# Differential attention's output turned one pass later, and sink attention's outputs in two banks

## The chip, the cores and the metric

The kernel runs on one core of one Trainium2 chip. The metric is the device time of one launch in microseconds; a kernel's time is the median of its runs. TensorE's clock is granted at 1.2 or 2.4 GHz, and the profile shows which; PEclk is its mean as a share of 2.4 GHz.

## The reference, cut to what matters

One inference step of a two-layer encoder over 1024 prompt tokens and 8 x 16 sample tokens, D = 1024. Layer 0 mixes differential attention (4 heads) and sliding-window attention with sinks (8 heads in 4 pairs), layer 1 is a chunk-band attention (16 heads in 8 pairs); each layer ends in a ConvFFN. What the change touches is in layer 0:

```
def diff_core(q, k, v, lam, mask):
    s = einsum('bqhcd,bkhcd->bhcqk', q, k) * ATTN_SCALE        # two score maps a head
    p = softmax(where(mask, s, NEG_INF))
    w = p[:, :, 0] - lam * p[:, :, 1]
    return einsum('bhqk,bkhe->bqhe', w, v)

def sink_core(q, k, v, sinks, mask):
    s = einsum('bqngd,bknd->bngqk', qg, k) * ATTN_SCALE
    p = softmax(concatenate([s, sink]))[..., :-1]              # a sink joins the denominator
    return einsum('bngqk,bknd->bqngd', p, v)

# even_mixer
oa = rmsnorm(oa, g_sub) * (1 - lam_init)                       # over a head's 128 columns
y = concatenate([oa, ob], axis=-1) @ w_out
```

All is float32; a matmul of two float32 operands is made of three, with high and low parts (`mm3`, `pair3`).

## The kernel before, in words

The program runs in blocks one after another: set-up with the adaLN projections, attention "AB" (layer 0), ConvFFN, attention "C" (layer 1), ConvFFN, final norm. Within a block each engine has its own instruction stream and waits on semaphores.

Attention handles one head (A, T = 0 to 3) or head pair (B, T = 4 to 7; C, T = 8 to 15) after another. I call them heads 0 to 7. For each, `tile_steps` writes out one list of steps, and every engine walks the same list and emits its part of each step in that order: the order of the list is each engine's order. The list goes in passes u = 0 to 8 over the eight 128-row blocks of queries, and then over the two groups of samples with cached keys (blocks 8 and 9). In pass u stand:

- FA(u-1): VectorE's softmax factors for the block before (L2089 to L2096 for A)
- S(u): scores (TensorE L1699 to L1708), drained by VectorE (L2036, or L2059 for B) and exponentiated by ScalarE (L1886)
- V(u-2): the value product into PSUM bank 7 (`mm3`, L86 to L88, for A; `pair3`, L116 to L118, for B). For A, ScalarE then evacuates it to `osb` (L1900) and squares `osb` (L1917, elementwise result to `osb2`, row sum to `ss`), and VectorE makes the mean (L1986)
- N(u-2), A alone: GpSimd raises the mean to the power -1/2 (L1475), and ScalarE scales `osb` by it into `osb2` (L1854)
- filler: matmuls of the next head's q, k and v projection (L86 to L88 with h and attAB_high), spread over the list
- T(u-1): transposes of the probabilities (L1611), cast by ScalarE to W (L1831), low part Wl by VectorE (L1970)
- O(u-2): for A, TensorE turns `osb2` (L1656, the turn) into columns 256 to 383 of bank 7, ScalarE scales it into `actr` (L1866), VectorE makes the low part `actl` (L1995). For B there is no turn; ScalarE copies out of bank 7 (L1870), VectorE makes the low part (L2000)

A value product waits until the output of the block before has left the bank (`o_bank_free`: `act_low` at least `un(T, u) - 1`). In the stream part, K steps transpose cached keys, and on GpSimd the same K steps issue the loads of cached values (L1372).

R steps are VectorE's rotations (L2020 to L2024) of the next head's q and k. At the end of each of the first seven heads SyncE stores its `actr` and `actl` to memory (L1315, L1316); when head 6 has been stored, six heads are read back into `h` and `hl` (L1325, L1326), and the output projection in head 7 waits for them.

Of the kernel before, what the change touches and what calls it, by code (L numbers as in the profile page):

```python
# [14 lines left out]
P = 128  # L15
# [991 lines left out]
def tile_steps(kind, T, fill, last, nxt):  # L1007
# [5 lines left out]
    late = 0 if fill == "q" else 1  # L1013
    for u in range(QB + 1):
# [7 lines left out]
        body += first + second + ([("V", u - 2)] if u > 1 else [])  # L1022
# [3 lines left out]
        body += ([("N", u - 2)] if u > 1 else []) + one + turned[0:2]  # L1026
        body += ([("O", u - 2)] if u > 1 else []) + two + turned[2:]
    body += [("LB",), ("V", QB - 1)]
    for g in range(2):
        u, x = QB + g, late if g else 1  # L1030
        body += [("K", g, 0), ("K", g, 1), 3 * x, ("N", u - 1), ("SK", g, 0), ("K", g, 2), ("O", u - 1), 2 * x,
# [63 lines left out]
def attention(nc, S, G, ins, outs, kinds):  # L1095
    ctx = ExitStack()
    with ctx:
# [47 lines left out]
        pair_o = ps[:, 7, 0:2 * P]  # L1145
# [101 lines left out]
        def probs_at(kind, T, u, p):  # L1247

            if u >= QB:
                n = 320 if kind == "A" else stream_width(kind)  # L1250
                return slice(0, n), t_banks[:, 0:n]
            n = min(512, (1 if kind == "A" else 2) * width(kind, u) - 512 * p)
            return slice(512 * p, 512 * p + n), ps[:, 5 + t_no(kind, T, u, p) % 2, 0:n]

# [78 lines left out]
        def _(pool):  # L1333
# [92 lines left out]
            def do(what, kind, T, s, c, turns):  # L1426
# [42 lines left out]
                elif what == "N" and kind == "A":  # L1469
# [34 lines left out]
        def _(pe):  # L1504
            spread_pe(pe, S, G, m, F["v"], rs, rs_s)

            def do(what, kind, T, s, c, turns):
# [66 lines left out]
                elif what == "SK":  # L1574
# [4 lines left out]
                    if b == 0:  # L1579
                        pe.wait_ge(S.qz, 2 * T + g + 1)  # L1580
                        pe.wait_ge(S.exps, s_no(T, QB + g - 1, 1 - g))
                    mm = mm3(pe, ps[:, 3, 0:nk], Qz[:, b, :], Qzl[:, b, :], kc[b % 2][:, 0:nk], kcl[b % 2][:, 0:nk],
# [30 lines left out]
                elif what == "V" and s[1] < QB:  # L1613
# [8 lines left out]
                    for j in range(nb):  # L1622
# [3 lines left out]
                        else:  # L1626
                            both, low = (t[:, 0:2 * nb * P].rearrange("p (z x) -> p z x", z=2)[:, :, x] for t in (W, Wl))
                            mm = pair3(pe, pair_o.rearrange("p (z x) -> p z x", z=2), v[:, y], vl[:, y], both, low,
# [23 lines left out]
                elif what == "O" and kind == "A":  # L1652
                    u = s[1]
                    rows = P if u < QB else 64
                    pe.wait_ge(S.o_rows, un(T, u))
                    pe.transpose(ps[:, 7, 256:256 + rows], osb2[0:rows, :], ident[0:rows, 0:rows]).then_inc(S.o_turned, 1)  # L1656
# [13 lines left out]
            def o_bank_free(kind, T, u):  # L1670

                pe.wait_ge(S.act_low, un(T, u) - 1)
# [77 lines left out]
        def _(act):  # L1750
# [12 lines left out]
            def do(what, kind, T, s, c, turns):  # L1763
# [91 lines left out]
                elif what == "O" and (s[1] < QB or kind == "A"):  # L1855
# [11 lines left out]
                    else:  # L1867
                        for z in range(2):
                            r = slice(HD * z, HD * z + HD)
                            i_ = act.copy(act_of(T)[0][r, lo:lo + P], pair_o[r, z * P:(z + 1) * P])  # L1870
# [22 lines left out]
            def outputs(kind, T, u):  # L1893
# [3 lines left out]
                act.wait_ge(S.probs, un(T, u))  # L1897
                if u < QB:
# [17 lines left out]
                if kind == "A":  # L1916
                    act.activation(osb2[0:rows, :], osb[0:rows, :], ACT.Square,  # L1917
# [14 lines left out]
        def _(dve):  # L1932
# [11 lines left out]
            def do(what, kind, T, s, c, turns):  # L1944
# [42 lines left out]
                elif what == "O":  # L1987
# [9 lines left out]
                    elif u < QB:  # L1997
                        for z in range(2):
                            r = slice(HD * z, HD * z + HD)
                            i_ = dve.tensor_tensor(al[r, u * P:(u + 1) * P], pair_o[r, z * P:(z + 1) * P],  # L2000
# [319 lines left out]
```

## Time and profile before

| | us |
|---|---|
| median of 3 runs | 3977.92 (3976.79 to 3984.57) |
| the profiled execution | 3989.37 |
| its span | 3987.8 |
| TensorE matmuls busy in it | 3534.9 (89%) |
| VectorE busy | 2122.8 (53%) |
| ScalarE busy | 1352.4 (34%) |
| mean granted clock | 0.924 |

One execution was profiled. PE is TensorE's matmuls, PEld its weight loads, DVE VectorE, ACT ScalarE, POOL GpSimd, SP SyncE. A time in brackets is the idle time of that engine before the instruction, with what ended it. The four A heads lie between about 240 and 800 us of the span, the B heads between 800 and 1120, the first ConvFFN up to about 2090, layer 1's attention up to about 3040.

### The profile page before, as it was taken

What the parts mean: (1) busy time and instruction counts of PE and PEld (TensorE: products, weight loads), DVE (VectorE), ACT (ScalarE), POOL (GpSimd) and SP (SyncE); (2) the same over time, 40 slices, a digit from 0 to 9 for tenths busy, and PEclk for the clock granted to TensorE, in tenths of its full rate; (3) what the DMA queues carried; (4) which work ended last, traced back from release to release, by engine and by line L of the source; (5) the groups of instructions that cost most, each with busy time, mean ns of one, the idle gap of its engine ahead of it and who ended that gap; (6) DMA issues with size and microseconds to landing.
All of it is one profiled execution on the core that took longest, in us unless ns stands there. A gap on an engine that the chain in (4) does not pass through costs nothing. (4 is left out here: it accounts for less than half of the span.)

```text
span 3987.8 us, 54257 instructions
## 1 busy us (share of the span) xinstructions
PE 3534.9 (89%) x20953; PEld 2087.5 (52%) x20953; DVE 2122.8 (53%) x3554; ACT 1352.4 (34%) x2665; POOL 485.6 (12%) x1018
## 2 busy tenths in 40 slices
PE   6878788877699999999988888888879999999997
PEld 3545455544464555555545555555546455555554
DVE  5654444455446555555555545545545655555555
ACT  6633444344223222122134444444432322212212
POOL 1012212222110000000010222211201000000000
PEclk8887888778799999999989999988989999999998
DMA  9722222211302111111111333333241211111111
GB/s 348 256 63 75 55 60 78 67 45 48 111 24 60 43 43 38 48 40 41 41 62 48 118 116 113 118 107 99 92 136 43 60 43 43 38 48 39 42 40 57
DMA packets 222127, 303.87 MB, mean 76 GB/s; under 512 B 24339, under 2 KB 174151, under 8 KB 221314
## 3 DMA queue, kind: packets, MB, share of 16 engines
q1 hardware_dynamic: 191938, 190.39, 14.7%
q0 software_dynamic: 30016, 111.15, 9.3%
q8 instruction: 112, 1.84, 0.2%
q14 instruction: 61, 0.50, 0.0%
HBM read 264.76 MB, written 63.95 MB: 82 GB/s over the span
## 5 line engine op out<-in xcount | busy, mean ns | idle before, releaser
L96 PE MATMUL psum<-h,ffn_high 128*128 128x512 f32 (+1 forms) x2016 | 989.1, 531 | 2.8 <-ACT u L858 2.8
L98 PE MATMUL psum<-hl,ffn_high 128*128 128x512 bf16 (+1 forms) x2016 | 616.2, 339 | 0.0
L100 PE MATMUL psum<-h,ffn_low 128*128 128x512 bf16 (+1 forms) x2016 | 562.9, 333 | 0.0
L96 PE MATMUL psum<-actr,ffn_high 128*128 128x512 f32 (+1 forms) x1056 | 518.1, 531 | 15.7 <-DVE actl L940 15.7
L96 PEld LDWEIGHTS psum<-h,ffn_high 128*128 128x128 f32 x2016 | 390.6, 194 | 82.9 <-ACT u L858 3.0
L98 PEld LDWEIGHTS psum<-hl,ffn_high 128*128 128x128 bf16 x2016 | 196.8, 98 | 412.8 <-issue 356.8
L86 PE MATMUL psum<-h,attC_high 128*128 128x384 f32 x744 | 365.1, 491 | 32.9 <-issue 16.5
L917 DVE TENSOR_SCALAR y<-u,cvT 128x1168 f32<-128x1168 f32 x88 | 78.2, 888 | 522.8 <-ACT u L863 522.8
L86 PE MATMUL psum<-h,attAB_high 128*128 128x384 f32 x648 | 329.4, 508 | 26.6 <-DMA hl<-act_low_dram 9.4
L98 PE MATMUL psum<-actl,ffn_high 128*128 128x512 bf16 (+1 forms) x1056 | 324.0, 340 | 0.0
L100 PE MATMUL psum<-actr,ffn_low 128*128 128x512 bf16 (+1 forms) x1056 | 295.7, 334 | 0.0
L177 ACT CAST ffn_high<-ffn_raw 128x1024 fp32r<-128x1024 f32 x132 | 139.3, 1055 | 441.4 <-PE psum L100 431.9
L857 ACT COPY u<-psum 128x1024 f32<-128x1024 f32 x88 | 89.3, 1015 | 522.5 <-PE psum L100 522.1
L87 PE MATMUL psum<-hl,attC_high 128*128 128x384 bf16 x744 | 265.1, 356 | 0.0
L88 PE MATMUL psum<-h,attC_low 128*128 128x384 bf16 x744 | 260.5, 350 | 0.0
L597 DVE SCALAR_TENSOR_TENSOR xT<-psum,mod,xT 128x1024 f32<-128x1024 f32 x192 | 245.3, 1277 | 0.0
L87 PE MATMUL psum<-hl,attAB_high 128*128 128x384 bf16 x648 | 241.0, 372 | 0.0
L88 PE MATMUL psum<-h,attAB_low 128*128 128x384 bf16 x648 | 236.4, 365 | 0.0
L96 PEld LDWEIGHTS psum<-actr,ffn_high 128*128 128x128 f32 x1056 | 205.7, 195 | 56.4 <-issue 16.7
L98 PEld LDWEIGHTS psum<-actl,ffn_high 128*128 128x128 bf16 x1056 | 103.5, 98 | 214.9 <-issue 186.0
L710 POOL COPY so<-u 128x2 f32<-128x2 f32 x88 | 18.1, 206 | 1569.7 <-ACT u L858 1569.7
L86 PEld LDWEIGHTS psum<-h,attC_high 128*128 128x128 f32 x744 | 151.9, 204 | 80.3 <-issue 40.0
(496 smaller groups left out, 7233.3 us busy)
## 6 DMA issues: line engine op xcount, KB each, us to landing
ada_raw<-in_ada_w SPq DMA_DIRECT2D x48, 1024.0 KB, 8.4
ffn_raw<-in_w_up SPq DMA_DIRECT2D x88, 512.0 KB, 3.8
ffn_raw<-in_w_down SPq DMA_DIRECT2D x44, 512.0 KB, 3.6
raw_C<-in_cache_c_k POOLq DMA_DIRECT2D x64, 256.0 KB, 3.9
raw_C<-in_cache_c_v POOLq DMA_DIRECT2D x64, 256.0 KB, 3.4
out_ck_s<-in_cache_c_k POOLq DMA_DIRECT2D x8, 1984.0 KB, 8.9
out_cv_s<-in_cache_c_v POOLq DMA_DIRECT2D x8, 1984.0 KB, 14.3
attC_raw<-in_w_in_odd SPq DMA_DIRECT2D x24, 512.0 KB, 5.6
```

Source lines behind the costliest of these rows:

```text
L86: pe.matmul(out, w, x, start=start, stop=False, skip_group_check=True)
L87: pe.matmul(out, top(w), xl, start=False, stop=False, skip_group_check=True)
L88: return pe.matmul(out, wl, top(x), start=False, stop=stop, skip_group_check=True)
L96: return pe.matmul(out, w, x[:, lo:hi], start=first and start, stop=last and stop, skip_group_check=True)
L98: return pe.matmul(out, top(w), xl[:, lo:hi], start=first and start, stop=last and stop, skip_group_check=True)
L100: return pe.matmul(out, wl, top(x[:, lo:hi]), start=first and start, stop=last and stop, skip_group_check=True)
L177: act.copy(self.w[s][:, :], self.raw[c % self.raws][:, :]).then_inc(self.high[s], 1)
L597: return dve.scalar_tensor_tensor(out=G.xT[:, n, 0:SEQ], in0=y[:, 0:SEQ], scalar=G.mod[:, a, 16 + n, 0:1], in1=G.xT[:, n, 0:SEQ], op0=ALU. ...
L710: pool.tensor_copy(so[:, 2 * g + j, 0:2], U[g][:, SEQ:SEQ + 2])
L857: act.copy(U[gate][:, 2:2 + SEQ], ps[:, 3 * gate:3 * gate + 2, :].rearrange("p b n -> p (b n)"))
L917: ch.then(dve.tensor_scalar(y[:, 0:n], u[:, 2:2 + n], cv[:, l, 2, bass.ds(f, 1)], cv[:, l, 3, bass.ds(f, 1)], ALU.mult, ALU.add))
```

## The change

For A, N moves from block u-2 to block u-3 and in front of V(u-2), and O moves from block u-2 to block u-3: the turn comes one pass later. GpSimd's power is issued at step V rather than N, right behind VectorE's mean. The squares' elementwise result goes to bank 7, columns 0 to 127, so `osb2` keeps its contents for a pass; the turn waits for the next block's squares. For B, even prompt blocks write bank 3 in place of bank 7. For A and B a value product waits for the output of two blocks before (`- 2`), not one. For C all is as it was.

```diff
@@ tile_steps
+    lag = 3 if kind == "A" else 2
-        body += first + second + ([("V", u - 2)] if u > 1 else [])
+        body += first + second + ([("N", u - 3)] if lag == 3 and u > 2 else []) + ([("V", u - 2)] if u > 1 else [])
...
-        body += ([("N", u - 2)] if u > 1 else []) + one + turned[0:2]
-        body += ([("O", u - 2)] if u > 1 else []) + two + turned[2:]
-    body += [("LB",), ("V", QB - 1)]
+        body += ([("N", u - 2)] if lag == 2 and u > 1 else []) + one + turned[0:2]
+        body += ([("O", u - lag)] if u >= lag else []) + two + turned[2:]
+    body += [("LB",)] + ([("N", QB - 2)] if lag == 3 else []) + [("V", QB - 1)]
...
-        body += [("K", g, 0), ("K", g, 1), 3 * x, ("N", u - 1), ("SK", g, 0), ("K", g, 2), ("O", u - 1), 2 * x,
+        body += [("K", g, 0), ("K", g, 1)] + ([("O", QB - 2)] if lag == 3 and g == 0 else []) + [3 * x, ("N", u - 1), ("SK", g, 0), ("K", g, 2), ("O", u - 1), 2 * x,
@@ banks
-        pair_o = ps[:, 7, 0:2 * P]
+        def pair_o(kind, u):
+            return ps[:, 3 if kind == "B" and u % 2 == 0 else 7, 0:2 * P]
@@ GpSimd
-                elif what == "N" and kind == "A":
+                elif what == "V" and kind == "A":
                     pool.wait_ge(S.ms, un(T, s[1]))
@@ TensorE, step SK, first of a group
+                        if kind == "B" and g == 0:
+                            pe.wait_ge(S.act_low, un(T, QB - 2))
@@ TensorE, step O
                     pe.wait_ge(S.o_rows, un(T, u))
+                    if u < QB - 1:
+                        pe.wait_ge(S.squares, un(T, u + 1))
+                    elif u == QB - 1:
+                        pe.wait_ge(S.act_low, un(T, u) - 1)
                     pe.transpose(ps[:, 7, 256:256 + rows], osb2[0:rows, :], ident[0:rows, 0:rows]).then_inc(S.o_turned, 1)
@@ o_bank_free
-                pe.wait_ge(S.act_low, un(T, u) - 1)
+                pe.wait_ge(S.act_low, un(T, u) - (2 if kind != "C" and 0 < u < QB else 1))
@@ ScalarE, step V
                 act.wait_ge(S.probs, un(T, u))
+                if kind == "A" and un(T, u) > 1:
+                    act.wait_ge(S.o_rows, un(T, u) - 1)
...
-                    act.activation(osb2[0:rows, :], osb[0:rows, :], ACT.Square,
+                    act.activation(ps[0:rows, 7, 0:P], osb[0:rows, :], ACT.Square,
                                    accum_out=ss[0:rows, :]).then_inc(S.squares, 1)
```

ScalarE in passes 3 and 4 of head 1, before: the evacuation (L1900), the squares (L1917), the scaling (L1854), the cast of the next probabilities (L1831), the scaled output (L1866).

```order
 L1886 ACTIVATE E_AB,st_AB<-E_AB,st_AB 128x512 x2
 L1900 ACTIVATE osb_AB<-psum,st_AB 128x128
 L1917 ACTIVATE osb_AB,fin_AB<-osb_AB 128x128
 L1854 ACTIVATE osb_AB<-osb_AB,fin_AB 128x128
 L1831 CAST W_AB<-psum 128x384
 L1866 ACTIVATE actr_AB<-psum,columns 128x128
 L1886 ACTIVATE E_AB,st_AB<-E_AB,st_AB 128x640 x2
```

The same passes now; the lines are ten to twelve further down.

```order
 L1896 ACTIVATE E_AB,st_AB<-E_AB,st_AB 128x512 x2
 L1864 ACTIVATE osb_AB<-osb_AB,fin_AB 128x128
 L1912 ACTIVATE osb_AB<-psum,st_AB 128x128
 L1929 ACTIVATE psum,fin_AB<-osb_AB 128x128
 L1841 CAST W_AB<-psum 128x384
 L1876 ACTIVATE actr_AB<-psum,columns 128x128
 L1896 ACTIVATE E_AB,st_AB<-E_AB,st_AB 128x640 x2
```

The scaling (L1864 now) stands in front of the evacuation and belongs to the block before it; nothing stands between the squares and the cast.

GpSimd at the end of head 0's prompt blocks, before: the power (L1475) of block 6, loads of cached keys and values (L1372), the power of block 7.

```order
 L1475 TENSOR_TENSOR fin_AB<-fin_AB,columns 128x1
 L1372 DMA E_AB<-in_cache_a_k 128x4x128 x2
 L1372 DMA raw_AB<-in_cache_a_v 128x4x128 x2
 L1475 TENSOR_TENSOR fin_AB<-fin_AB,columns 128x1
 L1372 DMA E_AB<-in_cache_a_v 128x4x128
```

And now (the power is L1479, the loads are L1376):

```order
 L1479 TENSOR_TENSOR fin_AB<-fin_AB,columns 128x1
 L1376 DMA E_AB<-in_cache_a_k 128x4x128 x2
 L1479 TENSOR_TENSOR fin_AB<-fin_AB,columns 128x1
 L1376 DMA raw_AB<-in_cache_a_v 128x4x128 x2
 L1376 DMA E_AB<-in_cache_a_v 128x4x128
```

The power of block 7 stands in front of the first two loads of cached values.

## Rows read from the trace of the kernel before

**Rows 1.** Windows, TensorE: stretch and its length, matmuls busy, granted clock, DMA.
```profile
388.00:521.60 133.60, 104.75 (x665) 0.86 0.25 69
656.00:793.30 137.30, 111.61 (x665) 0.80 0.23 67
240.00:800.00 560.00, 445.66 (x2738) 0.83 0.24 67
800.00:1035.00 235.00, 160.28 (x967) 0.81 0.16 45
2100.00:3000.00 900.00, 775.53 (x5122) 0.93 0.34 105
```

**Rows 2.** Waits of TensorE, 240 to 800 us: total us, times, longest.
```profile
PE psum L1656 <- ACT osb_AB L1854: 52.1, 29, 3.0
PE psum L1699 <- DVE st_AB L2036: 18.8, 16, 2.3
```

**Rows 3.** Timeline: turns of blocks 0, 1, 3, 7, 8 (head 1) and 2, 7 (head 2).
```profile
407.63 0.33 PE L1656 MATMUL psum<-consts,osb_AB 128*128 128x128 f32 x1 [2.60 <-ACT osb_AB L1854]
414.97 0.33 PE L1656 MATMUL psum<-consts,osb_AB 128*128 128x128 f32 x1 [2.33 <-ACT osb_AB L1854]
434.97 0.48 PE L1656 MATMUL psum<-consts,osb_AB 128*128 128x128 f32 x1 [2.99 <-ACT osb_AB L1854]
...
474.77 0.33 PE L1656 MATMUL psum<-consts,osb_AB 128*128 128x128 f32 x1 [1.87 <-ACT osb_AB L1854]
501.86 0.27 PE L1656 MATMUL psum<-consts,osb_AB 64*128 64x64 f32 x1 [1.18 <-ACT osb_AB L1854]
...
557.93 0.33 PE L1656 MATMUL psum<-consts,osb_AB 128*128 128x128 f32 x1 [0.47 <-ACT osb_AB L1854]
608.77 0.48 PE L1656 MATMUL psum<-consts,osb_AB 128*128 128x128 f32 x1 [2.56 <-ACT osb_AB L1854]
```

**Rows 4.** Timeline, pass 3 of head 1: from the squares' end to the scaling.
```profile
413.38 0.19 ACT L1917 ACTIVATION_READ_ACCUMULATOR osb_AB<-osb_AB 128x1 f32 x1
...
413.95 0.54 POOL L1475 TENSOR_TENSOR fin_AB<-fin_AB,columns 128x1 f32<-128x1 f32 x1 [6.80 <-DVE fin_AB L1986]
414.52 0.40 ACT L1854 ACTIVATE osb_AB<-osb_AB,fin_AB 128x128 f32<-128x128 f32 x1 [0.95 <-POOL fin_AB L1475]
```

**Rows 5.** Timeline, head 1: drain in pass 3, mean in pass 5, scores after.
```profile
410.62 0.69 DVE L2036 CUSTOM_DVE_ANT_0 E_AB<-psum,bm_AB 128x512 f32<-128x512 f32 x1 [0.89 <-PE psum L1708]
...
432.77 0.15 DVE L1986 TENSOR_SCALAR fin_AB<-fin_AB 128x1 f32<-128x1 f32 x1 [1.78 <-ACT osb_AB L1917]
...
440.09 0.69 PE L1699 MATMUL psum<-k_AB,q_AB 64*128 64x384 f32 x1 [0.75 <-DVE st_AB L2036]
```

**Rows 6.** Timeline of GpSimd, block 7 of head 0.
```profile
338.82 1.49 POOL L1372 DMA_DIRECT2D raw_AB<-in_cache_a_v  x2 [5.97 <-DVE kcl_AB L1980]
...
340.33 0.57 POOL L1475 TENSOR_TENSOR fin_AB<-fin_AB,columns 128x1 f32<-128x1 f32 x1
```

**Rows 7.** Waits of TensorE and of ScalarE, 800 to 1035 us.
```profile
PE psum L116 <- DVE actl_AB L2000: 29.6, 20, 5.9
...
ACT W_AB L1831 <- PE psum L1611: 13.7, 7, 4.5
```

**Rows 8.** Timeline, one pass of head 4: cast, low parts, next value product.
```profile
830.12 0.59 ACT L1831 CAST W_AB<-psum 128x512 fp32r<-128x512 f32 x1 [0.62 <-PE psum L1611]
...
830.74 0.69 DVE L1970 TENSOR_TENSOR Wl_AB<-psum,W_AB 128x512 bf16<-128x512 f32 x1 [2.33 <-ACT W_AB L1831]
...
831.35 0.58 DVE L2000 TENSOR_TENSOR actl_AB<-psum,actr_AB 64x128 bf16<-64x128 f32 x2
...
832.07 0.35 PE L116 MATMUL psum<-W_AB,v_AB 128*128 128x256 f32 x1 [0.89 <-DVE actl_AB L2000]
```

**Rows 9.** Timeline: the read back of six heads, and the first matmul on them.
```profile
1035.91 0.94 SPq L1325 DMA_DIRECT2D h<-act_high_dram  x1
...
1056.17 0.66 PE L86 MATMUL psum<-h,attAB_high 128*128 128x384 f32 x1 [9.42 <-DMA hl<-act_low_dram]
```

More of the change, by code:

```diff
@@ L1627, in do @@
                             both, low = (t[:, 0:2 * nb * P].rearrange("p (z x) -> p z x", z=2)[:, :, x] for t in (W, Wl))
-                            mm = pair3(pe, pair_o.rearrange("p (z x) -> p z x", z=2), v[:, y], vl[:, y], both, low,
+                            mm = pair3(pe, pair_o(kind, u).rearrange("p (z x) -> p z x", z=2), v[:, y], vl[:, y], both, low,
                                        j == 0, j == nb - 1)
@@ L1869, in do @@
                             r = slice(HD * z, HD * z + HD)
-                            i_ = act.copy(act_of(T)[0][r, lo:lo + P], pair_o[r, z * P:(z + 1) * P])
+                            i_ = act.copy(act_of(T)[0][r, lo:lo + P], pair_o(kind, u)[r, z * P:(z + 1) * P])
                     i_.then_inc(S.act_high, 1)
@@ L1999, in do @@
                             r = slice(HD * z, HD * z + HD)
-                            i_ = dve.tensor_tensor(al[r, u * P:(u + 1) * P], pair_o[r, z * P:(z + 1) * P],
+                            i_ = dve.tensor_tensor(al[r, u * P:(u + 1) * P], pair_o(kind, u)[r, z * P:(z + 1) * P],
                                                    ar[r, u * P:(u + 1) * P].bitcast(F32), ALU.subtract)
```

## The prediction

> **What bounds the kernel now.** I read the windows first, then TensorE's waits in each stretch, then single passes in the timeline. The windows [rows 1] put 560 us into the four differential heads (240 to 800), of which TensorE's matmuls fill 445.7, and 235 us into the sink heads 4 to 6 (800 to 1035), of which they fill 160.3. These two stretches are far from bound by TensorE's work. The rest of the span (the two ConvFFNs, layer 1) is not touched: the relevant code for layer 1 keeps its old order, bank and wait. So the question is what TensorE's idle time in 240 to 1035 turns into.
>
> In the differential heads the largest wait is L1656, the transpose that turns a block's normalised output: 52.1 us in 29 waits [rows 2]; all its 40 instances are in these heads. Behind it stand VectorE's draining of score banks (L1699, 18.8 us) and smaller ones. [rows 3] has the turn's waits in head 1 and three of head 2: 2.3 to 3.0 us where TensorE comes early, about 0.5 where its clock was low and it came late (the passes not shown have 0 where it came later still). The chain behind one is in [rows 4]: ScalarE's squares are complete at 413.57 (413.38 + 0.19), VectorE's mean follows, GpSimd's power starts at 413.95 and takes 0.54, ScalarE scales at 414.52 for 0.40, and the turn starts at 414.97 [rows 3]: 1.40 us from squares to turn. GpSimd and two engine crossings stand in a queue where nothing else can pass, since ScalarE has the cast of the next probabilities behind the scaling.
>
> In the sink heads the largest wait is the value product L116 for VectorE's low part of the block before, 29.6 us in 20 waits [rows 7]. The pass in [rows 8] shows why it is not worth 29.6: VectorE makes Wl at 830.74 for 0.69 (to 831.43), which the product needs too, and then the low part of the output, 0.58 from 831.35 to 831.93; the product starts at 832.07. Only the second of these goes.
>
> **The change, differential heads.** No instruction is added or removed but waits. The squares' elementwise result goes to bank 7 instead of osb2, so osb2 keeps the scaled block until its turn one pass later. The scaling now stands on ScalarE in front of the next block's evacuation and square; in rows 4 it takes 0.40. Nothing waits in front of it any more, but it delays the squares of that pass by about 0.35 (what lies between the scaling's start and the next start, estimated from its 0.40). The turn waits for those squares, since they write the same bank.
>
> The trace of before shows no ScalarE write of squares into PSUM. The nearest row is the scaling, 128x128 into SBUF, 0.40 [rows 4]; I bound the difference by a quarter of it either way, 0.1 a block, 4 us over the 40 blocks, and take 0. The Trainium skill (PSUM — Partial Sum Buffer, section on bank collisions) says that two engines may not touch one bank in the same partitions at a time, whatever the columns: that is what speaks against this use of bank 7. By that rule the turn must stay behind the squares, so the wait is shortened, not gone; TensorE is at the turn at 412.64 (414.97 less 2.33), 0.93 before the squares, and with the 0.35 the sum without that rule would have up to 1.3 more in each of the ten chain-bound passes below, 13 us. No run here shows a collision.
>
> So where TensorE comes early, the distance from squares to turn falls from 1.40 to about 0.05, and the squares are 0.35 later: 1.0 us gained per such pass. Passes, by number u of the scores in them:
> - Pass 2 loses its turn altogether (block 0 is turned in pass 3). TensorE saves 2.6 (407.63) [rows 3]; VectorE, which then drains the scores, had stood idle 0.89 for TensorE (410.62) [rows 5] and is rid of the chain's 1.40 in front of its own work. I take the smaller, 0.89 + 1.40 = 2.3, four heads: 9.2.
> - Passes 3, 4 and 7 of heads 0 and 1, passes 3 and 6 of heads 2 and 3: the chain bounds. 10 x 1.0 = 10.0.
> - Passes 4 and 7 of heads 2 and 3: TensorE was late and waited 0.5 to 0.6 (557.93) [rows 3]; the squares are ready even with 0.35 more. 4 x 0.55 = 2.2.
> - Pass 5: VectorE starts the rotation of the next head right after the mean (432.77) [rows 5], and TensorE then waits for the score drain behind it (440.09) [rows 5]. The 3.0 us wait of the turn (434.97) [rows 3] is therefore worth nothing, and the rotation starts 0.35 later: 4 x -0.35 = -1.4.
> - Pass 6 of heads 0 and 1: TensorE late, no wait, nothing.
> - Pass 8 has no scores; the cast of the last probabilities no longer stands behind GpSimd. Estimate 0.6 x 4 = 2.4.
> - Block 7: GpSimd's power stood behind two cache loads [rows 6]: the loads start at 338.82 and the power only at 340.33. The power is now in front of the loads, and with that the turn's waits of 1.87 and 2.56 (474.77, 608.77) [rows 3], 1.70 and 2.51 in the other heads go: 8.6. Block 6 is turned here, newly, behind the cache transposes and the squares of block 7: 0.2 each, 0.8. Net 7.8. The loads are then at most one power, 0.57, late; the score products of the cached keys, which come first, cover that, and without this cover it would cost 4 x 0.57 = 2.3.
> - Block 8: the same order on GpSimd. The remaining waits of about 2.0 in all (head 1's is 1.2) go.
>
> Sum: 9.2 + 10.0 + 2.2 - 1.4 + 2.4 + 7.8 + 2.0 = 32.2 us of the 52.1.
>
> **The change, sink heads.** Values of even blocks go to bank 3, and a product waits for the outputs two blocks before. What is left is the wait for Wl, 0.6 earlier. That is worth something only where TensorE's product sets the pass: where ScalarE waits for the transposes behind it (830.12, 0.62) [rows 8]. Rows 7 count 7 such waits in heads 4 to 6. Elsewhere ScalarE and VectorE run in a ring of their own (drain, exponentials, cast, Wl, output, factors), which the change does not shorten. With the last product of each of the three heads, behind which the cache transposes stand: 10 x 0.6 = 6.0. In head 7 nothing: the seven earlier heads' outputs are read back from memory from 1035.91 on, when head 6 has ended, and TensorE waits for them until 1056.17, with 9.4 us of idle time [rows 9]. What its first passes gain only lengthens that wait; but all that is gained before 1035 shifts the read too.
>
> **Clock.** Heads 1 and 3 run nearly the same work in 133.6 us at a granted clock of 0.86 and 137.3 at 0.80 [rows 1]; the clock is at one of its levels, 1.2 or 2.4 GHz, for stretches in each. That is 0.6 us per 0.01. Fewer idle gaps might lift the 0.83 of the four heads; I take 2 us out of bounds of -5 (0.02 down) and +25 (up to 0.93, the mean of layer 1's attention with its fuller TensorE).
> The Trainium skill (TensorE: Matmul & The Clock Gate, section on the clock gate) says that the gate follows how busy the array has been. The trace agrees in sign: 0.93 in layer 1's attention, where TensorE is 86% busy, 0.83 here at 80% [rows 1].
>
> Total: 32.2 + 6.0 + 2 = 40. The profiled execution took 3989.4 (span 3987.8), 11.5 above the median of the runs shown, 3977.9. Taken from its own time that is 3949; against the median, which the result is compared with, **3938 us**.
>
> **Rivals.**
> - *The waits move to the score drains (about 3959).* If VectorE's drains bound passes 3 to 8, those gain nothing. For it: 16 waits of L1699, up to 2.3 us, and pass 5 above. Against it: the cast that VectorE needs next stands on ScalarE behind the scaling, whose wait of 0.95 for GpSimd goes [rows 4]. Left are pass 2, block 7 and block 8: 9.2 + 7.8 + 2.0 = 19.
> - *The clock follows (about 3917).* The clock in the heads rises to layer 1's 0.93: 10 x 0.6 x 4 = 24 more, less what then waits for VectorE again; 21. For it: the 0.93 in [rows 1]. Against it: 16% of the time would still be idle, in gaps of 1 to 3 us.
> - *It does not do what it says (about 3977).* The squares come so late that the turn waits as before; pass 2 and the closing blocks' gain is eaten by cache loads that start later.
> - *Slower (about 3991).* The scaling in front of the squares lengthens the ring of every pass by 0.35, seven blocks in each of four heads: 9.8; and the gaps that move from one of 2.5 to two smaller ones take the clock down by 0.01 in the heads, 2.4, plus 1 for the waits on bank 3. It decides if ScalarE, and not GpSimd, is what each pass waits for, that is if VectorE gets its cast no earlier. Against it: ScalarE stood idle 0.95 in front of the scaling in rows 4.
>
> **How the numbers follow.** Forecast 0.58, drains 0.20, clock 0.12, no change 0.04, slower 0.06. The forecast's own spread (squares' write 4, clock 5, passes 3 to 8 by a third) is 3925 to 3952; the range goes to the drains on one side and the clock on the other: 3918 to 3963. A measurement tells 0.2%, 8 us, from no change. Faster 0.90, same 0.04, slower 0.06.
>
> **What would show it.** In the profile after: the turn's wait (L1656's line) falls from 52 to 10 to 18 us, and waits for ScalarE's squares are what is left; none in pass 2; none at blocks 7 and 8; the drain waits L1699 grow from 19 to some 25 to 30, most of it in pass 5; the product's wait in the sink heads falls from 30 to about 15 and names Wl; the wait for hl at the end of the attention is 9.5 to 11; layer 1 and the ConvFFNs keep their times. It would be wrong if L1699's wait took up most of the 52, or if ScalarE's cast did not come earlier after the squares.

## The result and the profile after

| | before | changed |
|---|---|---|
| median of the runs, us | 3980.79 (4 runs, 3976.79 to 3984.57) | 3932.36 (4 runs, 3929.32 to 3941.59) |
| ratio to before, 95% interval | | 0.9883 (0.9869 to 0.9898) |
| profiled execution, us (span) | 3989.37 (3987.8) | 3929.32 (3927.7) |

The changed kernel is 48 us faster, 1.2%. The forecast was 3938 with a range of 3918 to 3963. Between the two profiled executions lie 60 us, not 48: that of before was 8.6 above its median, that of after 3.0 below. Sums over the traces below are therefore larger than the gain that the medians show. The forecast of 40 us was taken from a first median of before, 3977.9; against 3980.8 the same 3938 is 43.

The stretches of the profile after, TensorE alone (stretch, length, matmuls busy, granted clock, DMA). The first line is head 1 from its predecessor's last turn to its own, the second all four differential heads, the third heads 4 to 6, the last one 900 us of layer 1's attention; they answer to [rows 1].

```profile
374.28:497.38 123.10, 99.64 (x665) 0.89 0.26 75
240.00:743.24 503.24, 407.46 (x2697) 0.89 0.25 72
743.24:978.34 235.10, 163.63 (x997) 0.83 0.18 50
2040.00:2940.00 900.00, 773.33 (x5151) 0.93 0.33 106
```

The same cuts in the kernel before, at its own times: 240 us to the last turn of head 3, and from there to the read-back.

```profile
240.00:793.31 553.31, 441.95 (x2709) 0.83 0.23 66
793.31:1035.91 242.60, 164.19 (x997) 0.81 0.17 49
```

Three readings. First, the differential heads are 50.1 us shorter and heads 4 to 6 7.5 shorter; together that is 57.6 of the 60. Layer 1's attention has its length, as forecast: 972.9 us before and 972.4 after, from the first to the last matmul of its projections. Second, of the 50.1, only 15.6 is idle time of TensorE (553.31 - 441.95 = 111.4, against 503.24 - 407.46 = 95.8). The other 34.5 us is the same matmuls taking less time (some records are missing, 12 more of them after, about 2 us): the granted clock rose from 0.83 to 0.89. With the levels at 2.4 and 1.2 GHz, a mean of 0.83 is about 34% of the stretch at 1.2 GHz, and 0.89 is 22%: some 188 us before, 111 after. Third, this split says where the time went and not what freed it. Where a chain through the other engines sets a pass, a quicker matmul only waits longer. What the clock is worth by itself takes an experiment, below.

The same heads in another execution show how firm these sums are. Heads 0 to 3 took 554.6 us with the banks alone, which has the old heads, and 504.9 in a second trace of the changed kernel. What lies behind the read-back, which no edit touches, took 2951.9 us in the trace of before, 2949.4 after, and 2940.1 to 2953.0 over all fourteen traces.

The waits of TensorE in the differential heads (total us, times, longest), which answer to [rows 2]:

```profile
PE psum L1709 <- DVE st_AB L2048: 36.0, 16, 4.8
...
PE psum L1666 <- ACT psum L1929: 12.6, 12, 1.7
```

The turn (L1656 before, L1666 now) waits 12.6 us and not 52.1, and what it waits for is named: ScalarE's squares. The wait for VectorE's score drain has nearly doubled, from 18.8 to 36.0. The turns of head 1 in the timeline (start, duration, instruction, idle time before and its releaser), which answer to [rows 3]:

```profile
398.05 0.30 PE L1666 MATMUL psum<-consts,osb_AB 128*128 128x128 f32 x1 [1.55 <-ACT psum L1929]
...
405.51 0.30 PE L1666 MATMUL psum<-consts,osb_AB 128*128 128x128 f32 x1 [1.39 <-ACT psum L1929]
...
415.58 0.27 PE L1666 MATMUL psum<-consts,osb_AB 128*128 128x128 f32 x1
...
451.56 0.30 PE L1666 MATMUL psum<-consts,osb_AB 128*128 128x128 f32 x1 [0.19 <-ACT psum L1929]
...
453.90 0.27 PE L1666 MATMUL psum<-consts,osb_AB 128*128 128x128 f32 x1
```

These are blocks 0, 1, 2, 6 and 7. Only three of ten turns wait in a head: 1.55 + 1.39 + 0.19 = 3.13, four times 12.5. The turn of block 7, which waited 1.87 [rows 3], does not wait.

The chain around the turn of block 0, which answers to [rows 4]:

```profile
397.72 0.19 ACT L1929 ACTIVATION_READ_ACCUMULATOR psum<-osb_AB 128x1 f32 x1
...
397.93 0.15 DVE L1998 TENSOR_SCALAR fin_AB<-fin_AB 128x1 f32<-128x1 f32 x1 [2.15 <-ACT psum L1929]
...
398.28 0.54 POOL L1479 TENSOR_TENSOR fin_AB<-fin_AB,columns 128x1 f32<-128x1 f32 x1 [4.61 <-DVE fin_AB L1998]
...
404.09 0.39 ACT L1864 ACTIVATE osb_AB<-osb_AB,fin_AB 128x128 f32<-128x128 f32 x1
```

The squares of block 1 end at 397.91 and the turn of block 0 starts 0.14 later, at 398.05, where 1.40 lay between a block's squares and its turn. GpSimd's power is ready at 398.82; the scaling that uses it runs at 404.09, without a wait.

The prediction said that it would be wrong if ScalarE's cast did not come earlier after the squares. Here is the cast behind the squares of block 1 of head 1, before and after:

```profile
414.83 0.46 ACT L1831 CAST W_AB<-psum 128x384 fp32r<-128x384 f32 x1
```

```profile
397.81 0.46 ACT L1841 CAST W_AB<-psum 128x384 fp32r<-128x384 f32 x1
```

It started 1.26 us behind the squares' end (413.57, [rows 4]) and now starts 0.10 before that end (397.91), so it comes some 1.3 us sooner after the squares. The scaling in front costs the squares 0.47, from its start (396.63) to that of the evacuation (397.10).

The last scores of pass 4, and then the pass with the rotation, which answers to [rows 5]:

```profile
410.59 0.38 PE L1709 MATMUL psum<-k_AB,q_AB 64*128 64x256 f32 x1 [2.14 <-DVE st_AB L2048]
...
415.43 0.15 DVE L1998 TENSOR_SCALAR fin_AB<-fin_AB 128x1 f32<-128x1 f32 x1 [2.27 <-ACT psum L1929]
415.50 1.22 DVE L2032 TENSOR_TENSOR f_q_AB<-f_q_AB,rope_AB 128x1024 f32<-128x1024 f32 x1
...
415.77 1.37 POOL L1479 TENSOR_TENSOR fin_AB<-fin_AB,columns 128x1 f32<-128x1 f32 x1 [7.25 <-DVE fin_AB L1998]
...
422.74 0.69 PE L1709 MATMUL psum<-k_AB,q_AB 64*128 64x384 f32 x1 [4.80 <-DVE st_AB L2048]
```

The turn (415.58, above) is past the gate at once, and TensorE then stands 4.80 us at the scores, behind VectorE, which has the rotation first. Before, the same place showed 2.99 at the turn [rows 3] and 0.75 at the scores [rows 5]: one wait swallowed the other, with 1.1 more. In heads 2 and 3 the turn had waited only 0.61 and 0.62 there, and the wait at the scores still grew, from 0.76 to 4.81 and from 0.80 to 3.64.

GpSimd at block 7 of head 0, which answers to [rows 6]: the power is now in front of the loads.

```profile
328.53 0.56 POOL L1479 TENSOR_TENSOR fin_AB<-fin_AB,columns 128x1 f32<-128x1 f32 x1 [4.50 <-DVE fin_AB L1998]
329.95 1.51 POOL L1376 DMA_DIRECT2D raw_AB<-in_cache_a_v  x2 [0.86 <-DVE kcl_AB L1992]
```

The sink heads 4 to 6, 743.24 to 978.34 us: TensorE's largest wait, ScalarE's wait for the transposes, and the pass of head 4 that [rows 8] has. They answer to [rows 7, 8].

```profile
PE psum L116 <- DVE Wl_AB L1982: 23.5, 20, 3.9
...
ACT W_AB L1841 <- PE psum L1617: 9.6, 4, 2.9
```

```profile
779.22 0.69 DVE L1982 TENSOR_TENSOR Wl_AB<-psum,W_AB 128x512 bf16<-128x512 f32 x1 [1.74 <-ACT W_AB L1841]
...
779.96 0.38 PE L116 MATMUL psum<-W_AB,v_AB 128*128 128x256 f32 x1 [1.62 <-DVE Wl_AB L1982]
```

The product starts 0.05 after Wl, where 0.64 lay before, and no longer waits for the output's low part. TensorE stands there 1.62 instead of 0.89: it is ready for the product earlier, and Wl sets its start.

The read-back, which answers to [rows 9], is 20.2 us from its start to the first matmul on it, as before, and the wait in front of that matmul is 9.92 (9.42 before).

```profile
978.34 0.92 SPq L1329 DMA_DIRECT2D h<-act_high_dram  x1
...
998.54 0.66 PE L86 MATMUL psum<-h,attAB_high 128*128 128x384 f32 x1 [9.92 <-DMA hl<-act_low_dram]
```

### The profile page after: what moved, and what is told of

It reads as the page before. It is cut to its first block and busy times, and to the rows that moved or that the text cites. A ratio compares the mean times of both kernels' runs of the same rounds, so it can differ in the third digit from the quotient of the medians.

```text
span 3927.7 us, 54293 instructions
## 1 busy us (share of the span) xinstructions
PE 3494.1 (89%) x20953; PEld 2068.2 (53%) x20953; DVE 2122.1 (54%) x3554; ACT 1350.6 (34%) x2665; POOL 486.9 (12%) x1018
## 3 DMA queue, kind: packets, MB, share of 16 engines
q1 hardware_dynamic: 191938, 190.39, 14.8%
## 5 line engine op out<-in xcount | busy, mean ns | idle before, releaser
L86 PEld LDWEIGHTS psum<-h,attC_high 128*128 128x128 f32 x744 | 151.5, 204 | 80.7 <-issue 40.2
## 6 DMA issues: line engine op xcount, KB each, us to landing
out_cv_s<-in_cache_c_v POOLq DMA_DIRECT2D x8, 1984.0 KB, 14.5
```

The costliest lines, as they stand in the source:

```text
L86: pe.matmul(out, w, x, start=start, stop=False, skip_group_check=True)
```

## Experiments

Twelve runs in three groups. A ratio is always to the kernel before, run beside it on the same chip. The kernel before stood at 3980.86 (20 runs), 3979.95 (7) and 3981.76 us (9) in the three groups. "Heads 0 to 3" is 240 us to the last turn of head 3, in the profiled execution.

### The two parts apart

Turn alone, on the changed kernel:
```diff
-            return ps[:, 3 if kind == "B" and u % 2 == 0 else 7, 0:2 * P]
+            return ps[:, 7, 0:2 * P]
-                pe.wait_ge(S.act_low, un(T, u) - (2 if kind != "C" and 0 < u < QB else 1))
+                pe.wait_ge(S.act_low, un(T, u) - (2 if kind == "A" and 0 < u < QB else 1))
@@ TensorE, step SK
-                        if kind == "B" and g == 0:
-                            pe.wait_ge(S.act_low, un(T, QB - 2))
```


> The changed kernel with its part for the sink heads taken back (one bank, a product waits for the output before); the later turn stays. Theory: the turn is most of it. In the two profiles the four differential heads together became 50 us shorter (240 to 793.3 before, 240 to 743.2 after) and the sink heads 7.5, so this one comes to about 3940, 40 to 42 us under the kernel before. Rival (the two parts need each other, since each shifts the stretch after it against the stores and loads): under 30 us. The granted clock in the differential heads is 0.89 as in the changed kernel, not the 0.83 of before.

Measured: 3934.99 us, 0.9885 (0.9871 to 0.9900).

Banks alone: on the kernel before, `pair_o` and the wait at step SK as in the change, and
```diff
-                pe.wait_ge(S.act_low, un(T, u) - 1)
+                pe.wait_ge(S.act_low, un(T, u) - (2 if kind == "B" and 0 < u < QB else 1))
```


> The kernel before with the part for the sink heads alone: even blocks in bank 3, a product waits for the output two blocks before. Theory: the product then waits for Wl, 0.6 us earlier, in some ten places: 6 to 7.5 us under before, about 3974. Rival: with the ring of VectorE and ScalarE the bound everywhere, no change, within 3 us.

Measured: 3975.09 us, 0.9991 (0.9979 to 1.0003). The stretch from the end of head 3 to the read-back, first with the turn alone, then with the banks alone:

```profile
747.72:987.44 239.72, 161.88 (x997) 0.83 0.18 49
```

```profile
794.62:1027.05 232.43, 159.92 (x997) 0.85 0.18 51
```

The turn is the change: alone it gives 46 of the 48 us. The bank makes heads 4 to 6 shorter in both traces, 235.1 against 239.7 with the turn and 232.4 against 242.6 without it, but in the medians it is 2.6 and 5.8 us, and an interval that reaches past 1.000. The traces of all runs without the rotation edit say more: this stretch took 239.5 to 242.6 us in the four that have one bank, and 231.9 to 237.5 in the seven that have two. So the two banks do shorten it, by some 6 us; the medians, with 2.6 and 5.8, do not resolve how much of that reaches the kernel's time.

### What the wait cost in order, and what it cost in clock

GpSimd's powers earlier, all else as before. It takes the powers out from behind the cache loads and leaves the turn in its old pass.
```diff
-                elif what == "N" and kind == "A":
+                elif what == "V" and kind == "A":
                     pool.wait_ge(S.ms, un(T, s[1]))
```


> The kernel before with one edit: GpSimd raises the mean to its power at step V in place of N, in front of the cache loads. The turn stays where it was. Theory of the prediction: blocks 7 and 8 lose the waits behind the loads, 8.6 + 2.0, so 10 us under before, about 3970. Rival (the profiles: from the squares of block 7 to those of block 9 the four heads gained 23.7 us together): 15 to 20 us, since the cast of the cached keys also stood behind the scaling on ScalarE, and the clock stays up.

Measured: 3963.42 us, 0.9955 (0.9940 to 0.9971).

The kernel before with matmuls in the gap: TensorE multiplies zero weights into the open accumulation of a projection while it would wait for the turn, 224 matmuls in all. No chain gets shorter, and TensorE has more work.
```diff
+            def keep_warm(count):
+                if mid[0] is not None:
+                    bank, k, lo, hi = mid[0]
+                    for _ in range(count):
+                        pe.matmul(ps[:, bank, 0:hi - lo], zero[:, :], hl[:, k, lo:hi], start=False, stop=False,
+                                  skip_group_check=True)
...
+                    if u < QB:
+                        keep_warm(8)
                     pe.wait_ge(S.o_rows, un(T, u))
```


> The kernel before, and in front of each turn of a prompt block (28 of the 32; in the others no accumulation is open) eight 128x384 bf16 matmuls with an all-zero stationary tile, added to an accumulation that is open, so that no result changes. They fill TensorE's wait for the scaled block with 1.3 us of work at 2.4 GHz, 2.6 us at 1.2 GHz. Theory (a good half of the change's gain is TensorE's clock: matmuls busy in the differential heads fell from 446 to 411 us between the profiles, idle time by 15 only): although work is added, this one is 5 to 15 us faster than before, with a granted clock over 0.86 in the heads. Rival (clock luck of one execution, the gain is waits alone): the clock stays near 0.83 and it is 5 to 20 us slower, by what sticks out of waits shorter than the added work.

Measured: 3968.06 us, 0.9968 (0.9954 to 0.9982). It adds 8 matmuls in front of 28 of the 32 turns of prompt blocks. The windows over heads 0 to 3, with powers first and with the gap filled:

```profile
240.00:776.04 536.04, 425.07 (x2710) 0.87 0.25 68
```

```profile
240.00:782.85 542.85, 448.21 (x2934) 0.90 0.24 67
```

The filled gap settles that the clock is a cause of its own. With 225 more matmuls on record in the stretch, the granted clock is 0.90 instead of 0.83, heads 0 to 3 are 10.5 us shorter, and the kernel 12.8 (medians). That is the least that the gaps at the turn cost in clock alone, since the time of the fillers is still in it.

The powers first take 17.3 us off heads 0 to 3 (17.4 in the medians), more than the 10.6 us of waits that the prediction put at blocks 7 and 8, and again the clock rises, to 0.87. TensorE's idle time did not fall at all, 111.0 against 111.4: the turn waits 19 times instead of 29, 45.2 us in all, TensorE stands elsewhere instead, and the whole gain is in the matmuls' time, 425.1 against 442.0. Most of it has one place. The stretch between the squares of blocks 7 and 8 took 25.4 to 28.2 us in the four heads before and takes 23.3 in all four, as in the changed kernel: 14.6 us together.

The reverse on the changed kernel: the powers of blocks 7 and 8 back behind the loads, all else as changed.
```diff
-                elif what == "V" and kind == "A":
+                elif kind == "A" and what in ("N", "V") and \
+                        what == ("N" if s[1] in (QB - 1, QB) else "V"):
```


> The changed kernel with the powers of blocks 7 and 8 put back to step N, behind the loads of cached values on GpSimd; all other powers stay at V. Theory: this undoes what the one-edit kernel (power first, otherwise as before) gained, 17 us, so about 3949; the turn's wait at block 7 comes back with 1.7 to 2.6 us in each of four heads. Rival (once the turn is a pass later the loads no longer matter): within 3 us of the changed kernel's 3932.

Measured: 3939.87 us, 0.9906 (0.9879 to 0.9933). On GpSimd at block 7 of head 1 the loads start at 458.42 and the power at 460.06. Its wait for the scaled blocks over heads 0 to 3, and its window:

```profile
PE psum L1667 <- ACT osb_AB L1865: 11.5, 8, 2.6
```

```profile
240.00:759.54 519.54, 415.45 (x2708) 0.88 0.25 70
```

Eight waits come back with 11.5 us, and the four heads are 16.3 us longer: 1.4 us for each us waited. 8.3 of it is idle time and 8.0 is matmuls at a lower clock. In the medians it is 7.5, 0.65 for each us waited, with intervals that overlap those of the changed kernel; so the order of powers and loads is worth 7 to 17 us by these measures, the direction is the same in all, and the size is not sharp.

The drains' gap filled: on the changed kernel, the same zero matmuls where TensorE waits for VectorE's drain (4, 8, 18 and 6 in passes 4 to 7).
```diff
+WARM = {4: 4, 5: 8, 6: 18, 7: 6}
...
+                                        if u > 3 and CUTS[x][2] == 512 and y == 0:
+                                            keep_warm(WARM.get(u, 0))
                                         cut_taken(pe, T, x - 3)
```


> The changed kernel with zero matmuls (as in the run on the kernel before) in front of the first wait for a drained score bank in passes 4 to 7 of the differential heads: 4, 8, 18 and 6 of them, in the 0.8, 2.1, 4.8 and 1.6 us that TensorE waits there. Theory (gaps cost clock too): the stretch at 1.2 GHz behind the rotation in pass 6 goes, 4 to 12 us under the changed kernel. Rival: the clock in the heads is already at 0.89 and these gaps cost none; same or slower, by up to 5 us.

Measured: 3935.18 us, 0.9877 (0.9843 to 0.9912). Its waits over heads 0 to 3, then its window:

```profile
PE psum L1679 <- ACT psum L1944: 25.1, 21, 1.7
...
PE psum L1724 <- DVE st_AB L2063: 9.9, 12, 1.6
```

```profile
240.00:753.66 513.66, 434.78 (x2844) 0.89 0.25 71
```

No gain: the drain wait falls from 36.0 to 9.9, the clock stays at 0.89, the heads are 10 us longer and the median is unmoved. Part of what the fillers hide at the drains comes back at the turn (25.1 instead of 12.6); in all, idle time fell by 16.9 and matmul time rose by 27.3. In these two runs, filling a gap paid where it raised the clock.

### The squares' bank

On the changed kernel, the squares' elementwise result into a scratch in SBUF instead of bank 7.
```diff
-                    act.activation(ps[0:rows, 7, 0:P], osb[0:rows, :], ACT.Square,
+                    act.activation(sqj[0:rows, :], osb[0:rows, :], ACT.Square,
```


> The changed kernel with the squares' elementwise result in an SBUF scratch tile (bf16) in place of bank 7; every wait stays. It tells what the write into PSUM is worth by itself: the instruction takes 0.281 us into PSUM and took 0.310 into SBUF before. Theory: 40 times 0.03, of which most is on the chain: up to 1 us slower, no change that can be measured. Rival (the write into bank 7 meets TensorE's or VectorE's use of the bank): 3 us or more faster.

Measured: 3922.88 us, 0.9865 (0.9834 to 0.9897), with heads 0 to 3 at 503.3 us, as long as in the changed kernel (503.2). So the 9 us are not where the squares are. Of the 12.4 between the two traces, 9.3 lie behind the read-back (2940.1 us against 2949.4) and 3.2 in heads 4 to 6, and the edit touches neither. I ran it again beside the unaltered changed kernel:

> The changed kernel, unaltered, as the common measure for the three beside it. The first comparison gave 3932.4 us and 0.9883 [0.9869, 0.9898]. Expected: 3929 to 3937 and 0.988 again.

Measured: 3932.75 us, 0.9877 (0.9861 to 0.9894).

> The changed kernel with the squares' elementwise result in an SBUF scratch instead of bank 7, once more beside the unaltered one. Three rounds gave 3922.9 with an interval of 0.6%, but the profile showed the differential heads as long as before the edit. My theory: no difference, within 0.2% of the kernel beside it; 4 us at most, since a square into PSUM took 281 ns and one into SBUF 310 ns in the traces. The rival, that the bank's sharing cost something: 8 to 10 us faster.

Measured: 3927.49 us, 0.9866 (0.9848 to 0.9884), 5.3 below its neighbour (0.13%), with overlapping intervals. Where the squares go makes no difference that these runs can tell; in the two groups the variant was 9.5 and 5.3 us below the changed kernel. The turn's wait for the squares is kept in this variant, so a kernel without that wait was not tried.

### The rotation in three

The one thing that the change left bound was the pass with the rotation. VectorE's three long steps of it are set apart, one in front of each of the next three value steps.
```diff
+    at = steps.index(("R", "q")) if ("R", "q") in steps else None
+    if at is not None and kind != "C":
+        vs = [i for i in range(at, len(steps)) if steps[i][0] == "V" and steps[i][1] < QB][0:3]
+        if len(vs) == 3:
+            for j in (2, 1, 0):
+                steps.insert(vs[j], ("R", "q", j))
+            del steps[at]
...
-            def rotate(name, nk, nT):
+            def rotate(name, nk, nT, parts=(0, 1, 2)):
...
```


> The changed kernel with VectorE's rotation of the next head's q cut into its three parts (two pairs of products of 1.5 us, a sum of 1.4), one in front of each of the next three V steps, where VectorE waits 2.2 us for the squares. Theory (the rotation in one piece is what bounds pass 5 and makes the 4.8 us wait for the score drain): that wait falls under 1.5, 3 to 4 us gained in each differential head and 2 to 3 in sink heads 4 to 6, 15 to 25 us in all, about 3912. Rival (ScalarE's exponentials or TensorE bound the pass right behind it): 3 to 8 us.

Measured: 3910.06 us, 0.9823 (0.9794 to 0.9852).

> The changed kernel with the rotation of q in three pieces, once more, now beside the unaltered changed kernel on the same chip. If the four passes with the rotation were held by the score drain behind it (my theory), 3910 comes again, some 20 us (0.5%) below the kernel beside it, 12 to 15 of it in the four differential heads. If the 3910 was chance among executions, the two agree within 0.2%.

Measured: 3908.35 us, 0.9819 (0.9802 to 0.9837), 24.4 us below the changed kernel on the same chip. It beats both kernels. The second run's waits over heads 0 to 3 and its window, and below them the scores of the same pass in the first run's head 1:

```profile
PE psum L1717 <- DVE st_AB L2061: 23.5, 16, 2.2
PE psum L1674 <- ACT psum L1937: 18.1, 17, 1.7
```

```profile
240.00:734.20 494.20, 408.69 (x2706) 0.88 0.27 73
```

```profile
419.34 0.44 PE L1717 MATMUL psum<-k_AB,q_AB 64*128 64x384 f32 x1 [1.50 <-DVE st_AB L2061]
```

The wait of 4.80 behind the rotation is 1.50, and the distance between the squares of blocks 3 and 4 is 39.0 us over four heads instead of 53.2 in the changed kernel beside it. Heads 0 to 3 are 10.7 us shorter and the stretch of heads 4 to 6, where the edit applies too, 4.6. That is 15.3 of the 24.4, where 12 to 15 were expected in the differential heads alone; 2.4 more lie behind the read-back, and the remaining 6.7 are in neither trace: the one of this run is 2.2 above its median, its neighbour's 4.7 below.

Why 14.2 us at the rotation leave 10.7 in the heads, the traces do show. The stretch between the squares of blocks 8 and 9, in head 0 of the kernel before, the changed kernel, and the rotation in three:

```profile
362.42:384.84 22.42, 20.60 (x132) 0.80 0.18 53
```

```profile
351.45:371.39 19.94, 18.54 (x132) 0.93 0.19 56
```

```profile
347.06:368.89 21.83, 20.45 (x132) 0.81 0.18 50
```

The changed kernel goes through it at 0.93 in all four heads, in both of its traces (78.9 us together in the one beside). The rotation in three falls back to 0.81 or 0.82 in three of the four heads and needs 84.7. So the clock took back 5.7 us there; over the four heads it is 0.88 against 0.89. Fewer idle gaps are not always a higher clock.

> Both edits at once: the rotation of q in three pieces, and the squares in SBUF. By my theory it takes what the rotation in three alone takes, within 0.2% (3910). By the rival of the bank's sharing it is 8 to 10 us below it, 3901.

Measured: 3909.34 us, 0.9811 (0.9794 to 0.9828), what the rotation in three takes alone. So the squares in SBUF add nothing here that can be told, and the rival that expected 8 to 10 us more is not borne out.

## Why the prediction was right, point by point

The forecast of 40 us against 48 was right in sign, and in what the turn waits for before and after; the sizes of the steps differ, and that the total is so close is in part luck. In the traces the stretches gave 57.6 where the sum has 40.2, and the medians show less because the trace of before was 8.6 us above its median and that of after 3.0 below. Gains of heads 0 to 3 are from one squares' end to the next in the two traces; these stretches add to the 50.1.

| step | predicted | in the traces |
|---|---|---|
| pass 2, turn gone | 9.2 | 12.4 |
| passes 3, 4, 6, 7 | 12.2 | 15.0 |
| pass 5, rotation | -1.4 | -2.5 |
| pass 8 | 2.4 | 0.2 |
| block 7 (squares of 7 to squares of 8) | 7.8 | 14.5 |
| block 8 (squares of 8 to squares of 9) | 2.0 | 9.2 |
| before the first squares, between heads, at the end | 0 | 1.3 |
| heads 0 to 3 | 32.2, and 2 of clock | 50.1 |
| heads 4 to 6 | 6.0 | 7.5 |
| read-back | 0 | 0 |

- **The turn's wait** was put at 10 to 18 us, naming the squares: 12.6. None in pass 2, none at blocks 7 and 8: so it is, and block 6's new wait, put at 0.2, is 0.19. The distance from squares to turn came out at 0.14, with 0.05 forecast.
- **Which passes wait** was half right. I let the chain bound up to four passes of a head; only the turns of blocks 0 and 1 wait over 1 us. In the later passes TensorE is held by the drains and comes to the turn late. The gain there came all the same: the cast, which VectorE needs next, comes some 1.3 us sooner after the squares, and 0.47 of that goes to the scaling in front.
- **Pass 2** was put at 2.3 a head. In two heads of before its stretch ran at full clock, and they gained 2.2 each; the other two ran at a lower one and gained 4.2 and 3.9. Here are heads 0 and 1 of before, from the squares of block 0 to those of block 1; after, the stretch takes 5.0 to 5.2 in all four heads, at 1.00:

```profile
270.85:280.20 9.35, 6.54 (x33) 0.82 0.00 1
```

```profile
406.22:413.57 7.35, 5.01 (x33) 1.00 0.00 1
```

- **The drains** were put at 25 to 30 us: 36.0. The step that failed is a plain one. I wrote that the turn's 3.0 in pass 5 is worth nothing, and yet did not add it to the drain's wait: 0.75 + 2.99 = 3.74, and with the later rotation and a quicker TensorE 4.80. The scaling in front of the squares delays that rotation by 0.47 and not by the 0.35 of the sum, which is part of why pass 5 lost 2.5 and not 1.4. In the four heads this wait is 4.61, 4.80, 4.81 and 3.64 where 0.75 to 0.80 stood: 14.8 of the 17.2 by which the wait grew. The rest is in pass 4 of heads 0 and 1, 2.14 where 0.71 stood (410.59, above).
- **Blocks 7 and 8** are terms that were mis-sized, by 7 us each. In head 1 the stretch between the squares of blocks 7 and 8 shows why. Before and after:

```profile
470.26:497.08 26.82, 19.18 (x125) 0.84 0.37 99
```

```profile
451.43:474.73 23.30, 17.44 (x126) 0.89 0.42 115
```

  It is 3.52 us shorter: 1.78 idle time, which is the wait of 1.87 [rows 3], and 1.74 matmuls at a higher clock. The sum had counted the first alone. At block 8 most is clock: 7.3 of the 9.2 us is matmul time, at 0.80 to 0.90 before and 0.93 after. The order of power and loads is the cause at block 7: its stretch takes 23.3 us in every head of the changed kernel and of powers first, and 25.2 to 28.2 in every head of the four traces that have the power behind the loads. The powers moved alone (17.3 us) and moved back alone (16.3 in the trace, 7.5 in the medians) stand against 9.8 forecast.
- **The clock** is the largest error. It is largely the same time as the excess at pass 2 and blocks 7 and 8, counted another way. I took 2 us and bounded it by 25. The clock rose by 0.06; by the prediction's own 0.6 us per 0.01 and head that is 14 us, which is most of the 16 by which heads 0 to 3 exceed the 34. The rule of the Trainium skill (TensorE: Matmul & The Clock Gate, section "Part 1: The HAM clock gate") that was cited there, that busyness sets the level, agrees with the filled gap: the clock went from 0.83 to 0.90 with nothing done but more matmuls. The rival "the clock follows" was thus half true, and its 3917 would have needed layer 1's 0.93.
- **Pass 8** got 0.2 and not 2.4: the cast that I saw released from GpSimd's power was not what the next squares waited for. ScalarE stood 3.21 us for the value product before them in the trace of before, and 2.95 in that of after. That was an estimate without a row, and it failed.
- **The squares' write into PSUM** was bounded by 4 us either way and taken as 0: that holds within what can be measured.
- **Sink heads**: 6.0 forecast, 7.5 in the traces, of which about 6 is the bank; the rest is within what this stretch varies from trace to trace without it (239.5 to 242.6). The product's wait was to fall to about 15 and name Wl. It names Wl and is 23.5: what one releaser gave free, the next one took, since TensorE came earlier to the same Wl. ScalarE's waits for the transposes, on which the term rested, fell from 13.7 in 7 to 9.6 in 4. The total came out, the row that was to show it did not.
- **Read-back, layer 1, ConvFFNs** kept their times.
- Why 3932 and not less, if the heads gave 16 us more: the two profiled executions are 60 apart where the medians are 48 apart. Where the 8.6 us lie by which the trace of before exceeds its median was not settled. Heads 0 to 3 do not show them (553.3, and 554.6 with the banks alone); heads 4 to 6 are the longest of four (242.6 against 239.5 to 241.3), and what lies behind the read-back is among the longest of fourteen.

Of the rivals, the drains (3959) failed although their wait did grow, because it grew by 17.2 where the turn's fell by 39.5, mostly where the turn's wait had stood, and passes 3, 4, 6 and 7, which that rival put at nothing, gained 15.0. "No change" (3977) failed: the turn waits 12.6 us for the squares and not 52. "Slower" (3991) failed: only pass 5 grew, by 2.5 over four heads.

## What to carry to other kernels

When a wait of 2 to 3 us stands in TensorE's queue among matmuls, price it twice: the idle time itself, and the matmuls behind it at the lower clock; here 11.5 us of waits put back cost 16.3 in the trace and 7.5 in the medians, and filling the gaps with work that computes nothing gained 12.8. A step that goes through another engine (a power, a norm's factor) can be consumed one pass later, when its scratch can be freed by putting the by-product of another instruction elsewhere. And before a wait is booked as won, look at the same engine's next wait: what stands behind the same releaser may take over the whole of it (2.99 + 0.75 became 4.80), and the gain lies in moving that releaser, here the rotation.

## What the runs showed of the hardware

GpSimd's power over 128x1 elements, 40 times in each kernel (duration ns: shortest, median, longest), in the kernel before and with the rotation in three:

```profile
L1475 POOL TENSOR_TENSOR fin_AB<-fin_AB,columns x40: 539/561/1370, 271.7 to 791.3; 128x1 f32<-128x1 f32 x40
```

```profile
L1487 POOL TENSOR_TENSOR fin_AB<-fin_AB,columns x40: 537/558/570, 270.6 to 731.4; 128x1 f32<-128x1 f32 x40
```

It takes 0.56 us, but 1.37 where VectorE has just begun a product of two 128x1024 SBUF operands (the rotation, 1.22 us), once in each differential head before and after: at 415.77 it started 0.27 after that product and ended 0.42 after it. With the rotation moved away no power takes more than 0.57. The Trainium skill (SBUF — State Buffer, section "SBUF: two separate sides") says that a VectorE instruction with two SBUF inputs and a GpSimd one that reads SBUF lock one another out for a whole instruction; by that rule the power waits for VectorE's end and then runs, and the trace agrees. It does not show the other side: VectorE's next product of this kind started at 416.83, before the power's end at 417.14, and took 1.22 us as well.

ScalarE's square of 128x128 took less time into PSUM than into SBUF, in the changed kernel and in the one before:

```profile
L1929 ACT ACTIVATE psum<-osb_AB x40: 274/281/283, 268.7 to 740.0; 128x128 f32<-128x128 f32 x32, 64x128 f32<-64x128 f32 x8
```

```profile
L1917 ACT ACTIVATE osb_AB<-osb_AB x40: 309/310/312, 270.4 to 790.5; 128x128 f32<-128x128 f32 x32, 64x128 f32<-64x128 f32 x8
```

That is 29 ns each, about 1.2 us over the forty, within the prediction's 4. On the changed kernel with the squares in SBUF it took 310 again. The Trainium skill (ScalarE: Activation LUTs, section "Step-by-step: what each stage is for") calls PSUM the quicker destination for ScalarE; the trace agrees.

The clock is not a function of idle time alone. The changed kernel had 95.8 us idle in heads 0 to 3 at 0.89, the powers first 111.0 at 0.87, the kernel before 111.4 at 0.83, and the rotation in three 85.5 at 0.88. What else sets it was not settled here.
